# Linear-attention level scores by halves of 64 tokens, and half of a 31-tap convolution on TensorE through diagonal matrices

## The reference

```python
def hybrid_mixer(h, ...):                      # h: 256 x 1024
    gq, gk, gv, gr, glr, ca, cg, sq, sk, sv = split(h @ w_in)
    # 1. gated linear attention: 4 heads, keys 32, values 64
    glog = log_sigmoid(glr @ w_gate2 + b_gate) / 16      # cumulated decay per key channel
    attn[i, j] = sum_d gq[i, d] * gk[j, d] * exp(b[i, d] - b[j, d])   for j <= i
    o_gla = rms(attn @ gv) * silu(gr)
    # 2. causal depthwise convolution, width 31, on 256 channels
    u = ca * sigmoid(cg)
    y = conv31(u, conv_w) + conv_b;  o_conv = silu(layer_norm(y))
    # 3. sliding-window attention: 8 query heads, window 128, sink logits
    return concat(o_gla, o_conv, o_swa) @ w_out
```

## Time and profile before

| | |
|---|---|
| median of 3 runs | 1563.89 us (1562.41 to 1565.69) |
| the profiled execution | 1561.05 us |
| its span, first to last instruction | 1559.0 us |
| its mean granted TensorE clock | 0.967 of full |
| TensorE busy | 1476.9 us, 95% |
| VectorE busy | 1025.6 us, 66% |
| GpSimd busy | 111.3 us, 7% |
| the mixers' time from unit 5 to the w_out units | about 739 to 816 us, and 1262 to 1339 us |

### The profile page before, as it was taken

One profiled execution on the slowest core, in us unless ns is written; L12 is line 12 of the kernel. 1 busy time (PEld: TensorE's weight loads), 2 busy tenths in 40 slices (PEclk: granted clock), 3 DMA queues, 4 the chain that ended last, 5 costly groups with the idle time before them and its releaser, 6 DMA issues. The chain is left out here.

```text
span 1559.0 us, 21130 instructions
## 1 busy us (share of the span) xinstructions
PE 1476.9 (95%) x8712; PEld 1295.9 (83%) x8712; DVE 1025.6 (66%) x1278; ACT 715.5 (46%) x892; POOL 111.3 (7%) x135
## 2 busy tenths in 40 slices
PE   6999999899999899998889999999999897999998
PEld 6999999799987788878777888878888786878886
DVE  6766786588855565555996666556654499765644
ACT  4433753455544544443345444454444334454433
POOL 0000000000000000000820000000000046000000
PEclk8999999899999999998979999999999997999999
DMA  7644465566654555454314655546655440465543
GB/s 261 210 134 137 141 205 172 165 176 185 189 189 162 177 187 189 162 176 109 109 51 152 211 186 184 189 143 222 189 176 186 111 136 28 142 206 176 190 152 107
DMA packets 254354, 256.13 MB, mean 164 GB/s; under 512 B 24483, under 2 KB 217268, under 8 KB 254260
## 3 DMA queue, kind: packets, MB, share of 16 engines
q1 hardware_dynamic: 253376, 252.21, 51.2%
q10 hardware_dynamic: 884, 2.58, 0.5%
HBM read 253.71 MB, written 1.05 MB: 163 GB/s over the span
## 5 line engine op out<-in xcount | busy, mean ns | idle before, releaser
L939 DVE TENSOR_TENSOR w_lo<-raw,w_hi 128x2048 fp32r<-128x2048 f32 x240 | 549.2, 2291 | 337.8 <-ACT w_hi L577 337.5
L577 ACT ACTIVATE w_hi<-raw 128x2048 fp32r<-128x2048 f32 x240 | 458.3, 1912 | 370.4 <-PE stream L1621 171.5
L1621 PE MATMUL stream<-a_hi,w_hi 128*128 128x256 f32 x1056 | 308.1, 292 | 11.6 <-DVE a_lo L958 8.0
L1621 PE MATMUL stream<-a_lo,w_hi 128*128 128x256 f32 x1056 | 304.9, 289 | 0.0
L1621 PE MATMUL stream<-a_hi,w_lo 128*128 128x256 f32 x1056 | 304.7, 289 | 0.0
L1621 PE MATMUL stream<-w_hi,a_hi 128*128 128x512 f32 (+2 forms) x672 | 254.9, 379 | 7.4 <-DVE w_lo L939 7.4
L1621 PE MATMUL stream<-w_hi,a_lo 128*128 128x512 f32 (+2 forms) x672 | 250.3, 372 | 0.0
L1621 PE MATMUL stream<-w_lo,a_hi 128*128 128x512 f32 (+2 forms) x672 | 249.6, 371 | 0.0
L1621 PEld LDWEIGHTS stream<-a_hi,w_hi 128*128 128x128 f32 x1056 | 209.3, 198 | 14.2 <-issue 8.6
L1621 PEld LDWEIGHTS stream<-a_lo,w_hi 128*128 128x128 f32 x1056 | 209.5, 198 | 0.0
L1621 PEld LDWEIGHTS stream<-a_hi,w_lo 128*128 128x128 f32 x1056 | 209.0, 198 | 0.0
(11 more groups left out here) (282 smaller groups left out, 1734.8 us busy)
## 6 DMA issues: line engine op xcount, KB each, us to landing
raw<-in_ffn_w_up SPq DMA_DIRECT2D x136, 512.0 KB, 5.0
raw<-in_ffn_w_down SPq DMA_DIRECT2D x104, 512.0 KB, 4.4
raw<-in_ffn_w_gate SPq DMA_DIRECT2D x88, 512.0 KB, 3.9
raw<-in_w_in SPq DMA_DIRECT2D x80, 512.0 KB, 4.7
raw<-in_w_out SPq DMA_DIRECT2D x24, 512.0 KB, 4.2
raw<-in_w_in SPq DMA_DIRECT2D x20, 256.0 KB, 4.0
raw<-in_w_ret_o SPq DMA_DIRECT2D x8, 512.0 KB, 4.0
raw<-in_w_lru_o SPq DMA_DIRECT2D x8, 512.0 KB, 4.3
```

The lines of the kernel that those rows point to most:

```text
L577: nc.scalar.activation(w_hi[s][:, :, :], raw[s][:, :, :], ACT.Copy).then_inc(w_hi_ready, 1)
L939: V.tensor_tensor(w_lo[s][:, :, :], raw[s][:, :, :], w_hi[s][:, :, :].bitcast(F32), ALU.subtract).then_inc(w_split, 1)
L1621: return nc.tensor.matmul(dst, lhs, rhs, start=start, stop=stop, skip_group_check=True)
```

## The change

Two things change in each of the two mixers, and the order of the instructions around them.

1. **Level scores by halves.** For levels 1 to 7 a valid pair lies in one half (64 tokens) of the block, so TensorE computes each level for keys and queries of the same half only: output partitions 0 to 63 or 64 to 127, 64 columns. Level 0 is computed for keys of the first and queries of the second half only. That makes 60 matmuls of 32x64 keys by 64 queries for a block in place of 32 of 32x128 by 128. All eight levels of all four heads of a block fit into the four banks at once, so there are two groups (one for each block t) instead of eight. VectorE takes level 0 with a plain copy of 64 partitions, the others with seven `copy_predicated` of 128x256. The masks shrink to 7x64 columns. The product with the values is split: 8 matmuls over keys 0 to 63 and 4 cross-block ones, then a wait of TensorE for its own last one (`near_done`), then 8 over keys 64 to 127 into the late 64 columns.
2. **The second feature tile by TensorE.** GpSimd multiplies the identity by each tap's weights: 31 matrices of 128x128 in `diag`, in the space of `b_hi` and `b_lo`, for layer 0 after the first block's FFN norm, for layer 1 after layer 0's w_out units. TensorE does 31 fp32 matmuls of `diag[:, tap]` by 256 columns of `up`, 8 before window scores 1, 8 before the level scores of block 0, 15 after unit 8. VectorE and GpSimd lose their taps of tile 1; VectorE adds the bias while reading `ps7`.
3. **Order.** VectorE does window scores 0 before the `qe` products; `read_pair(6)` before taps; taps are now 2 before window scores 1, 6 within each block's level scores, 17 at the end; `read_pair(8)` comes after the level scores of block 1. TensorE computes unit 8 in one piece between the level scores of blocks 0 and 1.

```diff
 PSM_SC, PSM_O, PSM_MEAN, PSM_VAR, PSM_1 = range(5)
-(PSM_SWA, PSM_GLA, PSM_CROSS, PSM_L) = (0, 2, 10, 11)
+(PSM_SWA, PSM_GLA, PSM_CROSS, PSM_L) = (0, 2, 4, 5)
 
 PS7_N0, PS7_SINK, PS7_1 = range(3)
-(PS7_RB, PS7_Z, PS7_PV, PS7_GBC, PS7_L) = range(5)
+(PS7_RB, PS7_Z, PS7_CONV, PS7_PV, PS7_GBC, PS7_L) = range(6)
...
     mask = np.zeros((LEV, P, P))
+    half = (a[:, None] // 64 * 64 + np.arange(64)[None, :])
...
-    return names, np.concatenate(parts, axis=1), mask.transpose(1, 0, 2).reshape(P, -1).astype(np.float32)
+    near = np.take_along_axis(mask[1:], np.broadcast_to(half, (LEV - 1, P, 64)), axis=2)
+    return names, np.concatenate(parts, axis=1), near.transpose(1, 0, 2).reshape(P, -1).astype(np.float32)
...
-        b_hi, b_lo = sb("b_hi", [P, KT, T], F32R), sb("b_lo", [P, KT, T], F32R)
+        bs = ExitStack()
+        b_hi, b_lo = sb("b_hi", [P, KT, T], F32R, scope=bs), sb("b_lo", [P, KT, T], F32R, scope=bs)
+        bs.close()
+        diag = sb("diag", [P, 32, P])
...
-        masks = sb("masks", [P, LEV, P], U8)
+        masks = sb("masks", [P, LEV - 1, 64], U8)
...
+            def diagonals(l, used):
+
+                pool.wait_ge(unit_used, used)
+                for tap in range(TAPS):
+                    at = VL["conv_w"] + 2 * tap + 1
+                    nc.gpsimd.tensor_tensor(diag[:, tap, :], ident, vecs[:, 2 + l, at:at + 1].broadcast_to([P, P]),
+                                            ALU.mult).then_inc(diag_ready, 1)
+
+            diagonals(0, USED[U1_UP - 1])
...
-                nc.gpsimd.memset(s_gla[:, :, :, :], 0.0).then_inc(zeroed, 1)
+                nc.gpsimd.memset(s_gla[:, :, :, 0:64], 0.0).then_inc(zeroed, 1)
...
-                pool.wait_ge(up_ready, l + 1)
-                products, sums = (TAPS - TAPS_DVE) * l, (TAPS - TAPS_DVE - 1) * l
-                for n in range(TAPS - TAPS_DVE):
-                    tap = TAPS_DVE + n
-                    at = VL["conv_w"] + 2 * tap + 1
-                    dst = y_tap[:, n % 2, :] if n else y_pool
-                    if n > 2:
-                        pool.wait_ge(tap_sum, sums + n - 2)
-                    nc.gpsimd.tensor_tensor(dst, up[:, 1, tap:tap + T], vecs[:, 2 + l, at:at + 1].broadcast_to([P, T]),
-                                            ALU.mult).then_inc(tap_product, 1)
-                    if n:
-                        pool.wait_ge(tap_product, products + n + 1)
-                        if n > 1:
-                            pool.wait_ge(tap_sum, sums + n - 1)
-                        nc.gpsimd.tensor_tensor(y_pool, y_pool, dst, ALU.add).then_inc(tap_sum, 1)
                 power_heads(8)
                 pool.wait_ge(centred_var, l + 1)
                 nc.gpsimd.tensor_tensor(rstd2[:, :], var2[:, :], mhalf[:, 0:1].broadcast_to([P, 2]),
                                         ALU.pow).then_inc(conv_rstd, 1)
                 tile_roots(True, True)
+                if l < LAYERS - 1:
+                    diagonals(l + 1, USED[U1_END + UL * l + UL_UP_B - 1])
                 tile_roots(True, l < LAYERS - 1)
...
 
                 def conv(steps):
-                    for tap, f in conv_steps[len(conv_at):len(conv_at) + steps]:
-                        n = 2 * tap + f
-                        acc, src, w = yc[tap % 2][:, f, :], up[:, f, tap:tap + T], vec("conv_w", n)
+
+                    for tap in range(len(conv_at), min(len(conv_at) + steps, TAPS)):
+                        acc, src, w = yc[tap % 2][:, 0, :], up[:, 0, tap:tap + T], vec("conv_w", 2 * tap)
                         if tap == 0:
-                            ins = V.tensor_scalar(acc, src, w, vec("conv_b", f), ALU.mult, ALU.add)
+                            ins = V.tensor_scalar(acc, src, w, vec("conv_b", 0), ALU.mult, ALU.add)
                         elif tap == 1:
                             ins = V.tensor_scalar(acc, src, w, None, ALU.mult)
                         else:
-                            dve.wait_ge(dve_chain, conv_at[tap - 2, f])
+                            dve.wait_ge(dve_chain, conv_at[tap - 2])
                             ins = V.scalar_tensor_tensor(out=acc, in0=src, scalar=w, in1=acc, op0=ALU.mult, op1=ALU.add)
-                        conv_at[tap, f] = mark(ins)
-
-                def gla_scores(n):
-
-                    t, heads = n // 4, slice(2 * (n % 2), 2 * (n % 2) + 2)
+                        conv_at.append(mark(ins))
+
+                def gla_scores(t):
+
                     dve.wait_ge(zeroed, 2 * l + 1)
-                    if n >= 2:
-                        dve.wait_ge(psm_free, psm0 + PSM_GLA + n - 1)
-                    dve.wait_ge(psm_full, psm0 + PSM_GLA + n + 1)
-                    for m in range(4):
-                        level = 4 * (n // 2 % 2) + m
-                        ins = V.copy_predicated(s_gla[:, t, heads, :], masks[:, level:level + 1, :].broadcast_to([P, 2, P]),
-                                                psm[:, heads, m * P:m * P + P])
-                        if m < 3:
+                    dve.wait_ge(psm_full, psm0 + PSM_GLA + t + 1)
+                    V.tensor_copy(s_gla[0:64, t, :, 64:P], psm[0:64, :, 0:64])
+                    for level in range(1, LEV):
+                        ins = V.copy_predicated(s_gla[:, t, :, 0:64], masks[:, level - 1:level, :].broadcast_to([P, GH, 64]),
+                                                psm[:, :, 64 * level:64 * level + 64])
+                        if level < LEV - 1:
                             written = mark(ins)
-                            if m == 1:
-                                conv(1)
+                            conv(1)
                             dve.wait_ge(dve_chain, written)
                     ins.then_inc(psm_free, 1)
-                    conv(1)
...
-                dve.wait_ge(up_ready, l + 1)
-                conv(3)
...
                 lo(cm + 6)
-                conv(3)
                 read_pair(5, qs[:, 0:2, :], SWD ** -0.5)
                 lo(cm + 7)
+                window_scores(0)
 
                 dve.wait_ge(group_evac, gm + 2)
                 for t in range(TT):
@@ -1506,11 +1496,10 @@
                                           qg[:, t * P:t * P + P].rearrange("p (o i) -> p o i", o=1).broadcast_to([P, LEV, P]),
                                           ALU.mult)
                 ins.then_inc(qe_ready, 1)
-                window_scores(0)
                 lo(cm + 8)
+                read_pair(6, qs[:, 2:4, :], SWD ** -0.5)
+                dve.wait_ge(up_ready, l + 1)
                 conv(2)
-                read_pair(6, qs[:, 2:4, :], SWD ** -0.5)
-                conv(6)
                 window_scores(1)
                 dve.wait_ge(psm_free, psm0 + PSM_SWA + 2)
...
-                for n in range(8):
-                    gla_scores(n)
-                    if n == 2:
-                        dve.wait_ge(ss_exp, l + 1)
-                        link(V.tensor_tensor(mx[:, 0, :], mx[:, 0, :], mx[:, 2, :], ALU.add))
-                        V.reciprocal(mx[:, 3, :], mx[:, 0, :]).then_inc(sums_ready, 1)
-                    if n == 1:
-                        dve.wait_ge(unit_used, USED[cm + 7])
-                        for t in range(TT):
-                            ins = V.tensor_scalar(vg[:, t, :], bank(7)[:, t * T:t * T + T], rs4[:, 2 + t:3 + t], None, ALU.mult)
-                        ins.then_inc(group_evac, 1)
-                    if n == 4:
-                        read_pair(8, gr[:, :, :], 1.0)
+                gla_scores(0)
+                dve.wait_ge(unit_used, USED[cm + 7])
+                for t in range(TT):
+                    ins = V.tensor_scalar(vg[:, t, :], bank(7)[:, t * T:t * T + T], rs4[:, 2 + t:3 + t], None, ALU.mult)
+                ins.then_inc(group_evac, 1)
+                dve.wait_ge(ss_exp, l + 1)
+                link(V.tensor_tensor(mx[:, 0, :], mx[:, 0, :], mx[:, 2, :], ALU.add))
+                V.reciprocal(mx[:, 3, :], mx[:, 0, :]).then_inc(sums_ready, 1)
+                gla_scores(1)
+                read_pair(8, gr[:, :, :], 1.0)
...
-                conv(len(conv_steps))
-                dve.wait_ge(dve_chain, conv_at[TAPS - 1, 0])
-                dve.wait_ge(tap_sum, (TAPS - TAPS_DVE - 1) * (l + 1))
-                V.tensor_tensor(yc[0][:, 1, :], yc[0][:, 1, :], y_pool, ALU.add)
-                link(V.tensor_tensor(yc[0][:, 0, :], yc[0][:, 0, :], yc[1][:, 0, :], ALU.add))
-                V.tensor_tensor(yc[0][:, 1, :], yc[0][:, 1, :], yc[1][:, 1, :], ALU.add).then_inc(yc_ready, 1)
+                conv(TAPS)
+                dve.wait_ge(ps7_full, ps70 + PS7_CONV + 1)
+                V.tensor_scalar(yc[0][:, 1, :], ps7[:, 0:T], vec("conv_b", 1), None, ALU.add).then_inc(ps7_free, 1)
+                dve.wait_ge(dve_chain, conv_at[TAPS - 1])
+                V.tensor_tensor(yc[0][:, 0, :], yc[0][:, 0, :], yc[1][:, 0, :], ALU.add).then_inc(yc_ready, 1)
...
-                    mm(psm[:, 3, 0:T], b_hi[:, 0, 0:P], b_hi[:, 0, :], True, True)
```

(92 more changed lines are left out.)

3 lines of the change are left out of this document (1 added, 2 removed).

## The result

| | before | after |
|---|---|---|
| median | 1563.15 us (4 runs, 1562.04 to 1565.69) | 1580.19 us (4 runs, 1575.0 to 1582.53) |
| ratio, 95% interval | | 1.0106 [1.0094, 1.0118] |
| profiled execution, its span | 1561.05, 1559.0 | 1575.0, 1573.2 |
| mean granted TensorE clock | 0.967 | 0.973 |
| GpSimd busy | 111.3 us | 57.8 us |

I forecast 1567.3, from 1558.5 to 1579. Slower was the likelier sign, but the reason was another. (The median before is here over one run more than the 1563.89 that the forecast starts from.)

What follows compares the result with a forecast made beforehand. VectorE was taken to bound the mixer, with TensorE standing still there. Terms: 2 x (0.4 + 1.3) + 0.3 - 0.3 = +3.4 us on 1563.89, giving 1567.3, range 1558.5 to 1579.

Steps and rivals of the forecast that it cites:

- GpSimd's products: Ahead of two FFNs: overlap with w_lo delays it by one product, up to 0.4 us each time; +0.3 taken.
- X: TensorE's level scores of one block, 120 records: 3.6 us taken, ends 1.6 and 6.2.
- four heads overlap: Rival on the level scores: X about 1.8, four heads overlapping instead of two; 1559.5 us, faster; chance 0.15.
- 2X - 6.8: Change per layer in the channel mean's start, from the new TensorE and VectorE order: +0.4 us at X = 3.6.
- X at least 3.0: Level scores of one block: 120 records starting at least 0.025 us apart; the sum would then end at 1564.9.
- Behind the channel mean: Split value product per layer: 16 more records and a TensorE wait, 0.8 to 1.3 us; 1.3 taken.
- shape changes drain TensorE: Rival in the value product: eight changes between 64 and 128 key rows, 3.3 us per layer; 1571.3 us; chance 0.12.
- +1.7: Per mixer: 0.4 up to the channel mean plus 1.3 behind it, slower.
- The clock behind the wait: After TensorE idles from 790.6 to 797.1: transposes at half-clock duration 2.82, value product's 16 records at 0.056 each.
- taps at 0.44 for 0.43: TensorE's convolution taps: 0.43 us for each 256-column tap, 13.3 us for 31.
- VectorE's two waits: VectorE waiting for psm twice in each mixer, 4 us and 9 us.
- Mask load: Kernel start: smaller mask load, 224 KB for 512, competes less with first weights; 0 to -0.7 us, -0.3 taken.

Runs made afterwards that it cites:

- Experiment 1: Kernel before plus only GpSimd's 31 products of 128x128 after the two norms that precede FFNs, nothing reading them: 1579.36 us, ratio 1.0106.
- experiment 3: Changed kernel with GpSimd waiting for its own previous product before each one: 1560.96 us, ratio 1.0009 to the kernel before.
- the 16 products of 8: Kernel before plus bursts of 16 GpSimd products in place of 31, nothing reading them: 1562.27 us, ratio 0.9995.
- experiment 9: Kernel before plus bursts of 62 GpSimd products of 128x64, no wait between them, nothing reading them: 1562.5 us, one execution.
- experiment 5: Changed kernel with read_pair(8) and 17 taps put ahead of VectorE's level scores of block 1: 1558.19 us, ratio 0.9978 to the kernel before.
- Experiment 4: Changed kernel with the value product's first 12 matmuls grouped by shape, eight of 64 keys first, then four cross-block: 1574.54 us, ratio 1.007 to the kernel before.
- experiment 6: Changed kernel with products one by one, value product grouped by shape, and read_pair(8) and 17 taps ahead of block 1: 1540.54 us, ratio 0.987 to the kernel before.

## Why the prediction was wrong, point by point

- **GpSimd's products: the step that failed.** "What overlaps `w_lo` can delay one by one GpSimd product, up to 0.4 us each time [...] 0 to +0.8 for both, I take +0.3." Start, length and what is idle ahead were right (31 x 0.36 = 11.2, in my 9 to 19). The unit of the delay was wrong: the rest of the burst, not a product. I had the rows for it: the splits ask 6.7 and 5.1 us behind the last root, into a burst of 9 to 19. (The 7.33 and 5.70 of the forecast are VectorE's whole idle time, which begins before the burst.) I did not ask what the worse case would give: 11.2 - 6.5 and 11.2 - 5.1, with the changed kernel's own times, so 4.7 and 6.1 us of wait. Measured: 4.5 and 5.9 on the splits (6.82 and 8.15 less 2.29), 6.7 and 7.5 on the FFNs with the clock. Experiment 1 shows it alone; the own wait of 3, the 16 products of 8 and the halves of 9 take it away. The rows that I had of GpSimd beside VectorE (taps of 0.83) are of a loop in which GpSimd waits for its own product before each sum; in experiment 3 such waits let VectorE in. They could not bound a loop without those waits. So the step was wrong in its mechanism; why VectorE got in at once in the second burst of experiment 5 and in experiment 9 stays open.
- **X.** 3.6 taken, 1.51 measured, just below my least bound of 1.6: the first rival, "four heads overlap", was right on the mechanism. With it the term is 2X - 6.8 = -3.8. Measured: unit 5 starts at 751.79 against 743.31, 8.48 later, and the channel mean at 810.11 against 805.71 + 8.48, so -4.1. The chain of terms holds; its size was off by 4.5. My estimate from the Trainium skill's floor of 25 ns between starts (TensorE: Matmul & The Clock Gate, "Wait — 56ns, not 53.3ns?"), X at least 3.0, is contradicted here: 100 records in 1.10 us. It counted records; counted by matmul, of two records each, the estimate is 60 x 0.025 = 1.5, against 1.51, though the first 50 came every 0.022.
- **Behind the channel mean.** 1.3 taken, 3.1 measured (4.55 against 1.5): the rival "shape changes drain TensorE", at its 3.3. Experiment 4 in its second mixer, and experiment 6, show 2.1 of it as the order of shapes. The remaining 1.0 is the 16 records more and the changes that are left, which no run parts. In sum -4.1 and +3.1 gave the mixer -1.2 and -0.5 where I had +1.7: two errors of opposite sign.
- **The clock behind the wait.** I costed the transposes at half clock and took the value product at full. In the changed kernel's profile it was so (0.85 and 1.00, below); in both mixers of experiment 3's profile and in the first of experiment 4's it was not, 6 to 7 us per mixer in experiment 3. It was not in my sum at all. It may carry most of the 5.2 between profile and median; that is argued from experiment 3's two groups of times and one profile, as only one execution of the changed kernel has a trace. Its windows:

```profile
808.00:813.00 5.00, 4.04 (x26) 2.40 (x25) 4.32 (x9) 2.21 (x4) 0.00 (x0) 0.85 0.02 3
813.00:818.00 5.00, 4.94 (x69) 4.09 (x70) 3.34 (x3) 0.63 (x1) 0.00 (x0) 1.00 0.55 152
```

- **Right:** taps at 0.44 for 0.43; VectorE's two waits in kind, if shorter than I had them (2.20 and 7.67 against 4 and 9); the wait ahead of block 1 as the place where the gain goes, shown by experiment 5.
- **Mask load.** Not resolved: the stretch ahead of FFN 1 varied from 515.96 to 519.56 over kernels with one code.

## What to carry to other kernels

A burst of GpSimd instructions that read SBUF, without waits among them, can be one block for a VectorE instruction with two SBUF inputs, as it was in nine of ten here. Let the worst case be what is left of the burst when VectorE asks, and put a wait on GpSimd's own last result into it, or end it before VectorE asks. What is moved "into idle time" has to fit into that idle time as a whole. And when an engine's order was written around an old bottleneck, look at which long wait the new order leaves in front of work that is ready: here moving `read_pair(8)` and 17 taps ahead of it was worth 8 us per mixer, where the change with its burst cured was level with the kernel before (experiment 3). Taken alone it made 22 us, 7 of them by the burst that happened to let VectorE in. And compare more than one execution: with one and the same kernel a mixer took 6 to 7 us more when the clock stayed down.

## What I had not expected of the hardware

- Four heads in four row groups, 32x64 by 64 columns: 0.011 us per record over the first 100 against 0.052, with a quarter of the keys times columns.
- A change between 64 and 128 key rows costs TensorE about 0.35 us at full clock (2.1 for six). At half clock it is about 0.6: the same twelve matmuls take 6.77 in experiment 3 (803.76 to 810.53) and 3.14 in experiment 4 (810.83 to 813.97).
- GpSimd products that wait for the one before come every 0.48, against 0.36; with the stops for VectorE's splits the burst is 22.66 in place of 11.14. The own wait costs only GpSimd's time.
